# Starting the sliding-window attention four rounds later than the delta-rule heads in a round-robin mixer schedule

## The reference, cut to what matters

```
o_a = sliding_window_attention(qa, ka, va, sinks)       # 8 heads of 64, window 128
o_b = gated_delta_rule(qb, kb, vb, g, beta)             # 4 heads of 128, chunks of 128 here
mix = concatenate([o_a, o_b]) @ w_out                   # w_out is "hwo" in the kernel
```

## Time and profile before

| | |
|---|---|
| median of 3 runs | 2356.04 us (2355.77 to 2357.68) |
| the profiled execution's own time | 2357.48 us |
| its span on the core | 2355.7 us |
| TensorE busy | 2310.6 us, 98% |
| DVE busy | 1426.6 us, 61% |
| ACT busy | 1075.2 us, 46% |
| POOL busy | 261.9 us, 11% |

### The profile page before, as it was taken

One profiled execution on the slowest core, in us unless ns is written; L12 is line 12 of the kernel. 1 busy time (PEld: TensorE's weight loads), 2 busy tenths in 40 slices (PEclk: granted clock), 3 DMA queues, 4 the chain that ended last, 5 costly groups with the idle time before them and its releaser, 6 DMA issues.

```text
span 2355.7 us, 31747 instructions
## 1 busy us (share of the span) xinstructions
PE 2310.6 (98%) x12936; PEld 1936.7 (82%) x12938; DVE 1426.6 (61%) x2188; ACT 1075.2 (46%) x1849; POOL 261.9 (11%) x235
## 2 busy tenths in 40 slices
PE   9988999999999999999989999999999999999997
PEld 7777988888888988888968888888887779888886
DVE  6797764434587753433775677636486446775455
ACT  5655363223367642322555654434254555444341
POOL 0041310000321400000520011100000000110000
PEclk9999999999999999999999999999999999999999
DMA  5220123333223232223221232332321112332221
GB/s 210 83 65 2 56 98 99 98 98 97 88 93 98 73 116 99 92 96 98 87 81 59 77 103 94 98 99 94 95 89 56 55 37 99 98 98 94 95 90 63
DMA packets 60641, 207.45 MB, mean 88 GB/s; under 512 B 7072, under 2 KB 9168, under 8 KB 60368
## 3 DMA queue, kind: packets, MB, share of 16 engines
q1 hardware_dynamic: 59856, 202.66, 26.3%
q0 software_dynamic: 640, 2.76, 0.3%
HBM read 201.93 MB, written 2.10 MB: 87 GB/s over the span
## 4 chain that ended last, share of the span: by engine, by line
PE 86%; DVE 9%; ACT 3%; issue 1%; DMA 0%; POOL 0%; SPq 0%; another core or an unknown queue 0%; DVEq 0%; ACTq 0%
PE ps L288 26%; PE ps L289 25%; PE ps L290 25%; DVE WL L261 1%; DVE TM L633 1%; DVE AR L858 1%; PE ps L2902 1%; PE ps L348 1%; PE ps L2931 1%; PE ps L350 1%; PE ps L349 1%; PE ps L2915 1%; DVE X L636 1%; PE ps L1841 1%; DVE XL L658 0%
## 5 line engine op out<-in xcount | busy, mean ns | idle before, releaser
L288 PE MATMUL ps<-XH,WH 128*128 128x512 f32 (+1 forms) x2120 | 794.4, 375 | 8.3 <-DVE WL L831 5.9
L290 PE MATMUL ps<-XH,WL 128*128 128x512 f32 (+1 forms) x2120 | 779.1, 368 | 0.0
L289 PE MATMUL ps<-XL,WH 128*128 128x512 f32 (+1 forms) x2120 | 779.0, 367 | 0.0
L261 DVE TENSOR_TENSOR WL<-RAW,WH 128x1024 fp32r<-128x1024 f32 (+1 forms) x378 | 462.3, 1227 | 177.9 <-ACT WH L249 177.2
L288 PEld LDWEIGHTS ps<-XH,WH 128*128 128x128 f32 x2120 | 400.2, 189 | 86.3 <-issue 8.8
L249 ACT ACTIVATE WH<-RAW 128x1024 fp32r<-128x1024 f32 (+1 forms) x378 | 386.7, 1035 | 153.4 <-DMA RAW<-in_w 123.6
L290 PEld LDWEIGHTS ps<-XH,WL 128*128 128x128 f32 x2120 | 400.2, 189 | 66.1
L289 PEld LDWEIGHTS ps<-XL,WH 128*128 128x128 f32 x2120 | 400.4, 189 | 64.9 <-issue 2.2
L288 PE MATMUL ps<-H,WH 128*128 128x512 f32 (+1 forms) x1200 | 431.1, 359 | 1.6 <-DVE AR L858 1.0
L289 PE MATMUL ps<-H,WH 128*128 128x512 f32 (+1 forms) x1200 | 429.7, 358 | 0.0
L290 PE MATMUL ps<-H,WL 128*128 128x512 f32 (+1 forms) x1200 | 429.6, 358 | 0.0
(11 more groups left out here) (424 smaller groups left out, 2319.7 us busy)
## 6 DMA issues: line engine op xcount, KB each, us to landing
RAW<-in_w SPq DMA_DIRECT2D x128, 512.0 KB, 3.3
RAW<-in_up SPq DMA_DIRECT2D x88, 512.0 KB, 3.3
RAW<-in_dn SPq DMA_DIRECT2D x32, 512.0 KB, 3.3
RAW<-in_hyb SPq DMA_DIRECT2D x20, 512.0 KB, 3.4
RAW<-in_qkv SPq DMA_DIRECT2D x18, 512.0 KB, 3.4
RAW<-in_kvf SPq DMA_DIRECT2D x17, 512.0 KB, 3.5
RAW<-in_rin SPq DMA_DIRECT2D x16, 512.0 KB, 3.3
RAW<-in_dn SPq DMA_DIRECT2D x16, 384.0 KB, 3.0
```

The lines of the kernel that those rows point to most:

```text
L261: dve.e.tensor_tensor(WL[:, s, 0:n], RAW[:, s, 0:n], f32(WH[:, s, 0:n]), ALU.subtract).then_inc(*w_lo.at(u))
L288: pe.e.matmul(out, wh, xh, start=first, stop=False)
L289: pe.e.matmul(out, wh, xl, start=False, stop=False)
L290: return pe.e.matmul(out, wl, xh, start=False, stop=last)
```

## The change

In the first four rounds the attention isn't asked for a step. Its step i therefore stands in round i + 4 instead of round i, on TensorE, DVE, ACT and POOL alike. No instruction is added or taken away, and no tile, size or semaphore changes.

```
+        ALONE = 4
+
         def hybrid_rounds(heads, att, ahead):
...
             over, rounds, left = set(), 0, 12
             while len(over) < 5:
-                for g in heads[0:2] + [att] + heads[2:4]:
+                for g in heads[0:2] + ([att] if rounds >= ALONE else []) + heads[2:4]:
                     if g not in over and next(g, "end") == "end":
                         over.add(g)
                 rounds += 1
                 if att in over and left and rounds >= 23:
                     ahead(2)
                     left -= 2
             ahead(left)
```

## The result

Over 20 executions each, the median went from 2357.24 to 2362.66 us (2355.77 to 2359.18 before, 2358.03 to 2364.49 after). The ratio is 1.0017, with a 95% interval of [1.0011, 1.0023], some 4.0 us on 2357.2. The medians alone differ by more, 5.4, since more than half of the executions of the changed kernel are of the slower of two kinds. The forecast was 2356.5 against a median of 2356.04, +0.5, with 2352.5 to 2361.5 as its range. +4.0 on 2356.04 is 2360.0 and lies in the upper part of that range; the difference of the medians would give 2361.46, just inside its end, and the median as measured, 2362.66, lies 1.2 above it. The measured change is several times the +0.5 that was forecast.

The account below looks back on a forecast made before the run. Bound: DVE in rounds 0 to 3, the attention's chain in 4 to 15, TensorE from 19. Lead -7.7 (+0.1, taken at 7.6), late rounds +7.7, clock +0.4: total +0.5, median 2356.5 us, range 2352.5 to 2361.5.

Parts of the forecast that it names:

- The front: Rounds 0 to 7: DVE sets the pace; round 3 ends 4.7 us earlier, round 7 7.7 earlier.
- The charge of 1.0 for POOL: Round 3: 1.0 us added to DVE's work because POOL still runs its products on Q.
- Rounds 8 to 15: With attention steps 4 to 11: no change of pace, a lead of 7.6 us kept.
- Rounds 16 to 22: With attention steps 12 to 18: a loss, 26.1 us instead of 18.4 to the end of u2.
- 7.7 more: Rounds 16 to 22: the extra us from attention steps, POOL's products and waits up to u2's end.
- Behind u2: TensorE's same instructions up to the first product needing a delta head, 18.01 us without a gap; norm 1.4 earlier.
- The clock: Idle TensorE from 155.8 to 164.9: a stretch at 1.2 GHz, mostly hidden, charged 0.4 us.
- Rival B: Front's low clock stays through rounds 5 to 7, beyond about 172: +5.4 us, 2361.9; chance 10%.
- C: Rounds 16 to 19 keep the attention's 17.8 us price, u and o matmuls on top: +4 to +6; chance 8%.
- A: Main forecast: front's gain given back at the back, +0.5 us, own range -3.5 to +4; chance 72%.
- D: u and o pieces fill the loop's gaps, POOL and DVE don't meet in round 3: -3.5 us or beyond; chance 10%.

Follow-up runs that it names:

- run 8: Changed kernel with POOL's eight products of round 16 cut to 32 of every 128 columns (outputs meaningless): 2357.75 us, 1.0005.
- run 2: Changed kernel plus 50 unused matmuls on TensorE in the idle front, ahead of the level-1 pieces: 2359.34 us, 1.0011.
- run 7: Changed kernel plus unused matmuls both in the idle front and ahead of six late value products of the attention: 2359.19 us, 1.0009.
- run 10: Attention two rounds behind instead of four, with unused matmuls in TensorE's front gaps and before scores of steps 1 and 2: 2358.05 us, 0.9998.

## Why the prediction was right, and where it was short

**The front: right.** First L1954 at 154.45 (154.7 predicted), DVE ending round 3 at 164.92 (164.9), round 7 at 180.71 (180.3). On DVE's timeline:

```profile
154.45 0.69 DVE L1954 TENSOR_TENSOR AR<-ps,COL 128x512 f32<-128x512 f32 x1 [1.49 <-PE ps L1834]
155.06 2.18 DVE L1957 TENSOR_TENSOR XF<-XF,Y 64x256 f32<-64x256 f32 x2
...
164.92 0.72 DVE L1968 TENSOR_TENSOR XF<-ps,Y 128x256 f32<-128x256 f32 x2
165.56 0.47 DVE L1701 TENSOR_REDUCE COL<-ps 128x1 f32<-128x128 f32 x2
...
180.71 0.72 DVE L1968 TENSOR_TENSOR XF<-ps,Y 128x256 f32<-128x256 f32 x2
```

The charge of 1.0 for POOL measured 1.35: two of L1957 took 2.18 beside POOL's last products on Q, and 0.83 in the next head.

**Rounds 8 to 15: right.** A period of four rounds is 17.97 and 17.63, shifted or not. The lead, counted from the first kq, is 7.14 at round 8 and 6.96 at round 16, where 7.6 was taken.

**Rounds 16 to 22: the mechanism right, the size short.** The term "7.7 more" measured 9.0 (27.43 against 18.44; 26.1 was predicted). Scores of blocks 12, 13, 14 and 15 start at 216.31, 221.40, 225.63 and 230.38; 216.2, 220.6, 224.6 and 229.4 were predicted. 0.8 is lost by block 13, where POOL holds not one but both operations on two columns:

```profile
218.10 0.98 DVE L1704 SCALAR_TENSOR_TENSOR COL<-VEC,COL 128x2 f32<-128x2 f32 x1
219.12 0.96 DVE L1706 TENSOR_TENSOR COL<-VEC,COL 128x2 f32<-128x2 f32 x1
```

In the kernel before only L1706 had it. With POOL's work cut, the 0.8 is back (run 8). Another 0.8 came behind the scores of block 15, where 11.8 us followed instead of 11.0; no run took that apart.

**Behind u2: right.** 18.08 us against 18.01, and the norm begins 11.9 after the end of u2 instead of 13.2 (1.4 earlier was predicted), at 254.1; 252 was predicted, with u2 ending 1.8 earlier than it did.

**The clock: the step that failed.** The forecast charged 0.4 for a stretch at the lower clock in front, and had TensorE at full clock through rounds 4 to 7, whose row has 0.83. The stretch came where predicted; finer windows put its ends at 160.1 and 170.4, and show TensorE at its full clock again:

```profile
170.60:170.90 0.30, 0.30 (x18) 0.30 (x14) 0.30 (x2) 0.11 (x2) 0.00 (x0) 1.00 0.00 0
```

TensorE's timeline has the last dense work ahead of it, the transposes that end at 155.7, and level matmuls inside the stretch:

```profile
152.07 3.66 PE L1834 MATMUL ps<-CST,AR 128*128 128x128 f32 x32
...
165.96 1.92 PE L1841 MATMUL ps<-XF,AR 64*64 64x64 f32 x32
```

1.92 for 32 of them, against 1.10 in the earlier trace rows. It costs the mixer 0.9 (run 2), which is part of why the lead is short: with the fillers the scores of block 4 start 0.9 earlier. What the forecast did not have is a second fall in rounds 16 and 17, worth 2.2 in the mixer of the one such execution that was profiled; 20 of the 42 executions of this kernel are of that kind by their clock. Rival B had the clock as its cause but at the wrong place: it asked for a low clock beyond 172 in rounds 5 to 7. The first kind's stretch ends at 170.4 and the second kind's at 171.2, so B did not occur. C came half true: it had the scores of block 15 at 230.2, and they came at 230.38, closer than the 229.4 of A. But its +4 asked for u2 at 244.6, which ended at 242.19. D needed POOL and DVE not to meet in round 3, where they did, and no loss beyond the predicted one in rounds 16 to 22, where it was larger.

**Sum.** In the mixer, a lead of 6.96, a loss of 8.99 and 0.07 behind u2 make +2.10, where the forecast had -7.6 + 7.7 + 0.4 = +0.5. The first kind of execution, whose mean over 22 is 2358.4 against 2357.2 for the kernel before, shows half of that; the place near 1200 gave 1.4 back in its profiles, against the one profile of the kernel before. The second kind, mean 2363.2, adds 2.2 and loses that 1.4 again where it was profiled. With half of the executions of each kind the mean is 2360.8, +3.6; the first measurement had 12 of 20 of the second kind.

That +4.0 fell inside the range is in part luck. A's own range ended at +4, for a further stall and 1.5 of clock, and the stated range went on to 2361.5 to take in B and C. The first kind alone is at +1.2, for the terms that were set too small; the rest comes with the second kind, whose fall of the clock in rounds 16 and 17 no term and no rival had.

Three things stay open: what makes one execution of the same program have the second fall and another not, what parts the executions of run 7, and what the three fastest of run 10 did.

## What to carry to other kernels

Delaying one chain against another on engines with fixed queues moves work, it does not remove any: look at the stretch that gets the chain's end, and count there what TensorE, already full, has to take. The price of a delay need not be monotonic; what seems to count is which light steps meet which heavy pieces. Try the neighbours (here the mixer with 1, 2 and 6 rounds was some 2 us shorter than with 4, in one profile each). Where a median moves by 0.2%, print the granted clock of each execution first: two kinds of execution make a median jump with their shares.

## What the runs showed of the hardware that was not expected

- The same program falls to 1.2 GHz at a second place in some executions and not in others: 20 of 42 by their mean clock, and in the one profiled 0.51 over 6.9 us, behind waits of 1.03 and 0.96 us among 64x64 matmuls. With the waits of those rounds filled, none of 11 executions was of that kind.
- With one gap filled, the fall was found later: in one profile each, the kernel before had 0.53 over 170.20 to 173.70; with that place filled, it had 0.50 over 221.40 to 228.00, on the path, and its mixer was 1.7 longer. That the filling is the cause is not shown.
- 10.2 us at half clock cost 0.9 us beside a full DVE. 3.5 us at the lower clock near 1200 cost some 1.4 us more behind TensorE's wait than ahead of it, in all of 14 profiles: ahead of it, the wait shrank from 3.79 to 2.19 us and ended no later.
